# Value products of wide attention steps as three products of rounded parts, with GpSimd's ropes spread over the steps

## What is computed

```python
proj = einsum('btd,dp->btp', x, w_in[l])          # split into a_q, a_k, a_v, b_q, ... i_w
o_a = chunked_relpos_attention(a_q, a_k, a_v)     # 9 chunks of 64 keys, learned bias
o_b = sliding_window_gqa_sinks(rope(b_q), rope(b_k), b_v, sinks)          # 2 chunks of keys, 2 key/value heads
o_c = differential_attention(rope(c_q), rope(c_k), c_v, lam)              # two softmax maps for each head
o_d = dsa_attention(rope(d_q), rope(d_k), d_v, rope(i_q), rope(i_k), i_w) # top 256 keys, one key/value head
mix = concatenate([o_a, o_b, o_c, o_d], -1)
x = layer_norm(ALPHA * x + mix @ w_out[l])
x = layer_norm(ALPHA * x + square(relu(x @ w_up[l])) @ w_down[l])
```

## Time and profile before

| what | us |
|---|---|
| three runs: lowest, median, highest | 2765.85, 2766.01, 2766.18 |
| profiled execution: span, first to last instruction | 2765.6 |
| TensorE busy (matmuls) | 2688.9 (97%) |
| VectorE busy | 1645.8 (60%) |
| GpSimd busy | 1262.5 (46%) |
| ScalarE busy | 998.6 (36%) |
| attention of layer 0, first to last exponent | 285.0 to 599.0 |
| attention of layer 1, first to last exponent | 1654.0 to 1968.7 |

### The profile page before, as it was taken

The page is one execution under the profiler, slowest core; times in us unless marked ns, Lnnn a source line. Parts: engine busy times, 40 slices in busy tenths (PEclk is TensorE's granted clock), DMA queues, the critical chain, the costliest instruction groups (busy, mean ns, idle before and its releaser), DMA issues.

```text
span 2765.6 us, 36226 instructions
## 1 busy us (share of the span) xinstructions
PE 2688.9 (97%) x12768; PEld 2102.4 (76%) x12768; DVE 1645.8 (60%) x3330; ACT 998.6 (36%) x2055; POOL 1262.5 (46%) x1170
## 2 busy tenths in 40 slices
PE   8999899999999999999999998999999999999997
PEld 7788467668788888888887875676787888888886
DVE  3787876635534355544959877776364534355448
ACT  2476454442222212222435654443422222212223
POOL 5433700014666556666364346001156566566661
PEclk9999899999999999999999999999999999999999
DMA  5311344523311111101152122355323101111102
GB/s 155 89 46 46 68 91 93 131 105 97 122 33 32 61 62 61 50 17 63 65 138 57 44 74 57 79 109 119 114 89 111 57 27 39 61 62 61 50 20 80
DMA packets 97418, 203.21 MB, mean 73 GB/s; under 512 B 14010, under 2 KB 23162, under 8 KB 96954
## 3 DMA queue, kind: packets, MB, share of 16 engines
q1 hardware_dynamic: 87800, 175.58, 23.5%
q10 hardware_dynamic: 9440, 25.33, 2.5%
HBM read 138.04 MB, written 8.61 MB: 53 GB/s over the span
## 4 chain that ended last, share of the span: by engine, by line
PE 87%; DVE 7%; issue 2%; DMA 2%; ACT 1%; SPq 1%; POOL 0%; ACTq 0%; DVEq 0%; POOLq 0%
PE ps L1276 8%; PE ps L1278 8%; PE ps L1277 8%; PE ps L1158 8%; PE ps L1301 7%; PE ps L1300 7%; PE ps L1302 7%; PE ps L942 4%; PE ps L943 4%; PE ps L944 4%; PE ps L1206 2%; PE ps L1208 2%; PE ps L1207 2%; PE ps L1133 1%; PE ps L1100 1%
## 5 line engine op out<-in xcount | busy, mean ns | idle before, releaser
L900 POOL TENSOR_TENSOR wlo<-wraw,whi 128x512 fp32r<-128x512 f32 (+2 forms) x336 | 444.7, 1324 | 202.1 <-ACT whi L1363 180.2
L898 POOL CAST whi<-wraw 128x512 fp32r<-128x512 f32 (+2 forms) x272 | 183.6, 675 | 740.2 <-DMA wraw<-in_w_out 289.4
L1276 PE MATMUL ps<-xhi,whi 128*128 128x512 f32 x1024 | 406.1, 397 | 0.0
L1278 PE MATMUL ps<-xhi,wlo 128*128 128x512 f32 x1024 | 405.9, 396 | 0.0
L1277 PE MATMUL ps<-xlo,whi 128*128 128x512 f32 x1024 | 405.9, 396 | 0.0
L2064 DVE TENSOR_TENSOR common<-common,ps 128x512 f32<-128x512 f32 x104 | 69.6, 687 | 460.4 <-PE ps L1302 459.9
L1301 PE MATMUL ps<-wlo,op_hi 128*128 128x512 f32 x784 | 311.7, 398 | 0.0
L1300 PE MATMUL ps<-whi,op_hi 128*128 128x512 f32 x784 | 309.5, 395 | 0.0
L1302 PE MATMUL ps<-whi,op_lo 128*128 128x512 f32 x784 | 308.0, 393 | 0.0
L1507 ACT ACTIVATE probT<-ps 128x512 f32<-128x512 f32 (+2 forms) x456 | 205.2, 457 | 240.4 <-PE ps L1142 73.8
L900 POOL TENSOR_TENSOR wlo<-down_raw,whi 128x512 fp32r<-128x512 f32 x168 | 226.2, 1349 | 98.7 <-ACT whi L1363 92.0
(11 more groups left out here) (249 smaller groups left out, 5495.4 us busy)
## 6 DMA issues: line engine op xcount, KB each, us to landing
wraw<-in_w_up SPq DMA_DIRECT2D x144, 256.0 KB, 3.1
down_raw<-in_w_down SPq DMA_DIRECT2D x112, 256.0 KB, 3.6
wraw<-in_w_in SPq DMA_DIRECT2D x80, 256.0 KB, 2.7
...
```

The lines of the kernel that those rows point to most:

```text
L900: nc.gpsimd.tensor_tensor(lo, loaded, hi.bitcast(F32), ALU.subtract).then_inc(S["w_lo"], 1)
L1276: mm(ps[:, b, :], wh, xhi[:, k, tok], start=(k == 0), stop=False)
L1278: last = mm(ps[:, b, :], wl, xhi[:, k, tok], start=False, stop=(k == KT - 1))
```

## The change

A step is *fine* when it is wide: width 4 in C, width 2 or more in A, B and D. That makes 148 of 228 steps: 84 of width 4 (48 in C, 12 in A, 24 in D), 20 of width 3 (12 in A, 8 in D) and 44 of width 2 (12 in A, 24 in B, 8 in D). For a fine step:

- ScalarE makes two exponents of the same scores instead of one: rounded, `p_hi` (fp32r), then `probT` (float32).
- GpSimd subtracts them: `p_lo = probT - p_hi`, in the place of `probT` (`rest`).
- TensorE issues three matmuls, `p_hi` by `v_hi`, `p_hi` by `v_lo`, `p_lo` by `v_hi`. The first two wait for `p_hi` and `v_lo`, the third for `p_lo`.
- The values' parts are made once for each of 11 value heads, 4 steps ahead: `v_hi` by ScalarE, `v_lo` by GpSimd, on 520 elements a partition.

With it, `LAG` goes from 2 to 3. GpSimd now walks through the steps in order: B's 18 rope operations stand one by one behind narrow steps of C (13, 14, 15, 21, 22, 23, and so on to 47), D's 24 one by one behind steps 97 to 120, and two slabs of w_out behind steps 208 and 214. The other slabs wait for the last value product, because `p_hi` and the parts of the values lie in the ring's places. The ring of slabs begins at place 0 in both layers, some semaphores are shared by the layers, and `junk` (what VectorE writes beside the maxima) is bfloat16.

```diff
 def ring(l, n):
-    return (l * SLAB_LAST + n) % RING
+    return n % RING
...
-LAG, TURN_LAG = 2, 6
+LAG, TURN_LAG = 3, 6
...
+def fine(n):
+
+    job, _, a, b, _, _, _ = STEPS[n]
+    kind = HEADS[JOBS[job][0]][0]
+    return kind in FINE_KINDS and b - a >= (4 if kind == "C" else 2)
...
+NARROW = [n for n, z in enumerate(STEPS) if HEADS[JOBS[z[0]][0]][0] == "C" and not fine(n) and z[0]]
+ROPE_B = NARROW[0:18] if "C" in FINE_KINDS else []
+ROPE_D = list(range(FIRST_STEP[2 * H] + 1, FIRST_STEP[2 * H] + 25)) if "C" in FINE_KINDS else []
+WEIGHTS_AT = [N_STEPS - 20 + 6 * j for j in range(2)]
...
+            def rest(n):
+
+                job, _, a, b, _, _, _ = STEPS[n]
+                kind, w = HEADS[JOBS[job][0]][0], P * (b - a)
+                pool.wait_ge(S["p_done"], n + 1)
+                nc.gpsimd.tensor_tensor(p_lo[n % 4][:, 0:w], probT[n % 4][:, 0:w], p_hi[p_place(n)][:, 0:w].bitcast(F32),
+                                        ALU.subtract).then_inc(S["p_lo"], 1)
...
+                for n in range(N_STEPS):
...
+                    for v in v_split_at(n):
+                        values_lo(v)
+                    if fine(n):
+                        rest(n)
+                    if "C" in FINE_KINDS and n == FIRST_STEP[2]:
+                        clear_last_slot(n + 1)
+                    if n in ROPE_B:
+                        call, op = divmod(ROPE_B.index(n), 6)
+                        turn_b(call, [op])
+                    if n in ROPE_D:
+                        call, op = divmod(ROPE_D.index(n), 6)
+                        turn_d(call, [op])
+                    if n in WEIGHTS_AT:
+                        weights(SLAB_OUT + WEIGHTS_AT.index(n))
...
-                pe.wait_ge(S["p_done"], n + 1)
...
+                v = V_OF[hd]
+                hi, lo = v_hi[v_place(v)][:, kt, :], v_lo[v_place(v)][:, kt, :]
+                pe.wait_ge(S["v_lo"], passed(l, "v_lo") + v_done(v))
+                pe.wait_ge(S["p_hi"], passed(l, "p_hi") + fine_done(n))
+                mm(ps[0:HD + 1, 5 + turn % 2, at_q], hi, p_hi[p_place(n)][:, 0:w], start=fresh, stop=False)
+                mm(ps[0:HD + 1, 5 + turn % 2, at_q], lo, p_hi[p_place(n)][:, 0:w], start=False, stop=False)
+                pe.wait_ge(S["p_lo"], passed(l, "p_lo") + fine_done(n))
+                mm(ps[0:HD + 1, 5 + turn % 2, at_q], hi, p_lo[n % 4][:, 0:w], start=False, stop=end).then_inc(S["pv_done"], 1)
...
+                if fine(n):
+                    kind = HEADS[JOBS[job][0]][0]
+                    nc.scalar.activation(p_hi[p_place(n)][:, 0:P * (b - a)], ps[:, 2 + n % 2, 0:P * (b - a)], ACT.Exp,
+                                         scale=SCALE[kind]).then_inc(S["p_hi"], 1)
```

More of the change, by code:

```diff
@@ L519, in build @@
         r += 16 * SEQ
+        bias_at = r
         bias_a = tensor("bias_a", [P, H, 2 * P], F32, r)
@@ L527, in build @@
         r += 4 * P + 256
-        probT = [tensor(f"probT{j}", [P, W], F32, r + 4 * W * j) for j in range(3)]
-        probT.append(tensor("probT3", [P, W], F32))
+        prob_at = [r + 4 * W * j for j in range(3)] + [region(4 * W)]
+        probT = [tensor(f"probT{j}", [P, W], F32, prob_at[j]) for j in range(4)]
+        p_lo = [tensor(f"p_lo{j}", [P, W], F32R, prob_at[j]) for j in range(4)]
         assert r + 12 * W <= R1 + 8 * D_MODEL * TILES
@@ L692, in place_free @@
             elif prev:
-                done, value = RELEASE[SLAB_LAST + n - RING]
+                done, value = RELEASE[max(z for z in range(SLAB_LAST) if ring(0, z) == ring(l, n))]
                 engine.wait_ge(prev[done], value)
@@ L832, in fill, with turn @@
                 then(nc.gpsimd.memset(dst.bitcast(F32), value))
-            def turn(v, heads, cs, half, t0, nt):
+            def turn(v, heads, cs, half, t0, nt, ops=range(6)):
                 v = v.rearrange("p t (h s d) -> p t h s d", s=2, d=half)
@@ new lines, in turn, with turn_b @@
+                if 5 in ops:
+                    then(nc.gpsimd.tensor_tensor(b, b, w, ALU.add))
+            def turn_b(call, ops=range(6)):
+                if call < 2:
+                    turn(block(B_Q, BLK, 4 * call, 4), 4, cs64, HD // 2, 4 * call, 4, ops)
+                else:
+                    turn(block(B_K, P), 2, cs64, HD // 2, 0, TILES, ops)
+                if call == 2 and 5 in ops:
+                    nc.gpsimd.memset(zero_p[:], 0.0).then_inc(S["pool_roped"], 1)
+                    pool.wait_ge(S["pool_roped"], 2)
@@ new lines, in turn_d, with quiet @@
+            def turn_d(call, ops=range(6)):
+                turn(raw_d[:, 2 * call:2 * call + 2, 0:5 * HD], 5, cs64, HD // 2, 2 * call, 2, ops)
+                if call == 3 and 5 in ops:
+                    nc.gpsimd.memset(zero_p[:], 0.0).then_inc(S["pool_roped"], 1)
+                    pool.wait_ge(S["pool_roped"], 3)
+            def quiet(n):
+                if fine_done(n - 1):
+                    pool.wait_ge(S["p_lo"], passed(l, "p_lo") + fine_done(n - 1))
+                v = max([v for z in range(n) for v in v_split_at(z)], default=-1)
+                if v >= 0:
+                    pool.wait_ge(S["v_lo"], passed(l, "v_lo") + v_done(v))
@@ new lines, in clear_last_slot, with clear_keys @@
+            def clear_last_slot(n):
+                pool.wait_ge(S["qk_ready"], 8)
+                quiet(n)
+                fill(stacks[2][3][HD:96, :], 0.0)
+                nc.gpsimd.memset(stacks[2][2][HD:96, :].bitcast(F32), 0.0).then_inc(S["ones_set"], 1)
+                pool.wait_ge(S["ones_set"], 1)
+            def clear_keys(n, slot, hd):
+                pool.wait_ge(S["st_ready"], FIRST_STEP[2 * hd + 2])
+                quiet(n)
+                nc.gpsimd.memset(stacks[slot][3][HD:96, :].bitcast(F32), 0.0).then_inc(S["ones_set"], 1)
+                pool.wait_ge(S["ones_set"], 2 + slot)
@@ L907, in gpsimd_layer @@
                     t_sum(z[0], "T2" if z[1] == 1 else "T4", k)
+            for n in range(N_SLABS):
+                if n == STACK_SLAB:
+                    beside_attention(weights)
+                if not SLAB_OUT <= n < SLAB_OUT + len(WEIGHTS_AT):
+                    weights(n)
         def tensor_layer(pe, l, S, prev):
@@ L1152, in pv @@
                 job, kt, a, b, half, fresh, end = STEPS[n]
-                kind, h = HEADS[JOBS[job][0]]
+                hd = JOBS[job][0]
+                kind, h = HEADS[hd]
                 turn = 2 * job + half
-                pe.wait_ge(S["p_done"], n + 1)
+                at_q, w = slice(P * (a - 4 * half), P * (b - 4 * half)), P * (b - a)
                 if turn >= 2:
                     pe.wait_ge(S["o_evac"], turn - 1)
-                mm(ps[0:HD + 1, 5 + turn % 2, P * (a - 4 * half):P * (b - 4 * half)], values(kind, h, kt),
-                   probT[n % 4][:, 0:P * (b - a)], start=fresh, stop=end).then_inc(S["pv_done"], 1)
+                if not fine(n):
+                    pe.wait_ge(S["p_done"], n + 1)
+                    mm(ps[0:HD + 1, 5 + turn % 2, at_q], values(kind, h, kt), probT[n % 4][:, 0:w], start=fresh, stop=end
+                       ).then_inc(S["pv_done"], 1)
+                    return
+                v = V_OF[hd]
[6 more added lines that the diff above has]
+                mm(ps[0:HD + 1, 5 + turn % 2, at_q], hi, p_lo[n % 4][:, 0:w], start=False, stop=end).then_inc(S["pv_done"], 1)
             def turn_out(turn):
```

126 lines of the change are left out of this document (83 added, 43 removed).

## The result

The changed kernel takes **2848.7 us** (median of 4 runs, 2843.9 to 2849.8) where the kernel before takes 2766.1 in the same session: a ratio of 1.0291, with a 95% interval of 1.0279 to 1.0304. It is slower by 82.6 us, where the forecast was 2778, in a range that ended at 2804. The side was right, the size was not.

The account below looks back on a forecast made before the run. The prediction took TensorE to bound the kernel. Its terms, savings and delays together, summed to +6.2 us a layer, +12.4 for both, on 2766.0: 2778 us, likeliest case 2772 to 2792, full range 2752 to 2804.

Parts of the forecast that it names:

- What bounds the kernel now: Whole kernel: the time is TensorE's, so an edit pays by what it takes from TensorE, unless another engine replaces it.
- What a value product costs TensorE: Fine steps: three fp32r products cost 0.70 us against 0.86 at width 4; 18.9 us a layer saved in all.
- Steps 0 to 47: First half of C: GpSimd's ropes, v_lo and p_lo make step 48 start late, +7.5 us, between +2 and +11.
- Steps 48 to 95: Second half of C: TensorE's saving comes through only in part, -0.5 us for four jobs, between -3.8 and +3.
- VectorE beside a busy GpSimd: Attention from step 48 on: VectorE slowed 0.3 us in 7 of 16 jobs, +2 us a layer, between 0 and +8.
- Steps 96 to 119: First part of A: GpSimd's ropes of D and p_lo delay step 120, +4.9 us, between +2 and +8.
- Steps 120 to 143: Rest of A: GpSimd has room, so TensorE's saving stays, -1.9 of 2.1 us.
- B: Head group B: -1.0 of 1.7 us, since TensorE waits there and a step's chain grows.
- D: Head group D: GpSimd's work fits, so TensorE's saving stays, -4.8 of 5.3 us.
- LAG 3 at nothing: Attention: the longer lag costs nothing; it removes waits of TensorE that the busy row has no room for.
- VectorE is held out further: Rival, ends of C, A and D jobs: VectorE waits for GpSimd, 10 us a layer more, 2798 us; chance 0.07.
- TensorE falls to the lower clock: Rival, steps 12 to 47: waiting for GpSimd lowers TensorE's clock, 11 us a layer, 2800 us; chance 0.06.

Follow-up runs that it names:

- no_rest: The changed kernel without GpSimd's p_lo subtractions, the third product reading p_hi again: 2767.5 us.
- fine_none: The changed kernel without any three-product step; LAG 3 and the w_out slabs rounded inside D stay, ropes stand ahead of the loop: 2772.8 us.
- both_light: no_rest with one product and one exponent in wide steps, and the maxima of C and A over half the columns: 2733.1 us.
- Unwaited: The changed kernel with GpSimd still making every p_lo, but TensorE's third product reading p_hi and not waiting for it: 2842.4 us.

## Why the prediction was wrong

**What bounds the kernel now: in part wrong.** I read a TensorE that is busy 58.3 of 61 us in the second half of C as a TensorE whose savings pay. In D that was right. In C it was not: in no_rest TensorE has the saving (2658.0 us busy in all, 2688.9 before), and C takes 127.8 us instead of 122.3. Of these 5.5 us fine_none, which has the lag without the products, shows 1.4 (2.6 of 3.4 in layer 1). That TensorE was busy did not say that its work paced the stretch; what does is open, since C kept its 125 us too when VectorE was relieved together with the others (both_light).

**What a value product costs TensorE: right.** 0.70 us against 0.86 in D. D gained 5.8 us against 4.8, but that is partly luck: 1.2 of it is the lag, which I had at nothing (76.0 us in fine_none), and 4.6 are the products. And of 18.9 us a layer only D's part came through in any run with three products.

**Steps 0 to 47: +7.5, measured +12.5, the mechanism only in part.** GpSimd was busy 59.6 of 73.5 us there, 81%, not over 90%, and TensorE's idle time was ended by VectorE (12.3 us, 5.0 before) and hardly by `p_lo` (1.5). Without TensorE's wait for `p_lo` the stretch still takes 70.9, and without the subtractions 64.6.

**Steps 48 to 95: -0.5, measured +18.2. This is the step that failed.** Its sum held TensorE's products, ScalarE's exponents and GpSimd's 6.9 us, each for itself, and for VectorE one clause, that it "has little room either". GpSimd's 40 us of work were costed by whether they fit, not by whom they hold out. I had the row for it: the earlier trace rows show 1.28 against 0.34 us. TensorE waited 16.0 us for VectorE in this stretch, 2.6 before, and 1.5 for `p_lo`.

**VectorE beside a busy GpSimd: +2, measured about +29.** (That is the growth of TensorE's waits for VectorE in a layer, from 12.7 to 41.3 us. Unwaited less no_rest, 2842.4 - 2767.5 for two layers, gives 37, but holds ScalarE's 9.8 us of waits for GpSimd and the lower clock.) This is the term that was mis-sized, and the same error seen from the other side. I took 0.3 us in 7 of 16 jobs, from the one operation before each turn of the maxima. VectorE's instructions grew by 35.2 us a layer, because more than a dozen kinds of operation are concerned (bias parts, scans and selections of D's keys, the subtraction of the second map), six to nine of them close together at the end of many jobs, where TensorE waits for the last.

**Steps 96 to 119: +4.9, measured +9.6.** The queue that I worked out is there: TensorE waited 5.7 us for `p_lo` and 2.7 for VectorE. Unwaited takes back 2.8, but ScalarE waited for GpSimd in its place. What the forecast lacked here is that VectorE's scans hold GpSimd too, 1.7 us in the longest of these waits.

**Steps 120 to 143: -1.9, measured +6.5**, with 5.3 us of waits for VectorE and none for `p_lo`; **B: -1.0, measured -0.4** (+1.6 in layer 1); **D: -4.8, measured -5.8**, right in kind and nearly in size.

**LAG 3 at nothing: wrong by 6 us in all** (fine_none). And TensorE was to be busy less in all: it was busy 2691.7 us instead of 2688.9, with a granted clock of 0.83 and 0.90 in C where it had been 0.94 and 1.00; in no_rest it was 2658.0.

**The side, slower, is partly luck.** The two terms that made it, +7.5 and +4.9, were the queue for `p_lo`, which in these stretches shows as 1.5 and 5.7 us of waits; most of what made the kernel slower lay in the two terms that I had at -0.5 and +2.

**The rivals.** "VectorE is held out further" had the mechanism, and a chance of 0.07 at +10 us a layer. What I held against it, that most of VectorE's work reads PSUM, is true by count and beside the point: the operations that read SBUF stand together at the end of a job, on the path. "TensorE falls to the lower clock" (0.06, 11 us a layer) happened as well, for 16 us in all by the estimate above, but behind waits for VectorE more than behind those for GpSimd.
